# Two-part gather and scatter in the experts, earlier expert loads, and a modulation in halves, in a two-block transformer kernel

## The reference

```python
sh1, sc1, g1, sh2, sc2, g2 = split(silu(c) @ w_mod + b_mod, 6)        # and the same for c_ctx
hx = rmsnorm(x, norm_attn_g) * (1 + sc1) + sh1                        # hc: the same of ctx
proj = hx @ w_in                                                      # queries, latents, keys, values
x = x + g1 * (attention over 256 context and 256 own tokens) @ w_out
t = rmsnorm(x, norm_ffn_g) * (1 + sc2) + sh2
combine = softmax weights of the 2 best of 4 experts in the best of 4 groups, 0 elsewhere   # [256, 16]
hid = silu(t @ w_gate[e]) * (t @ w_up[e])                             # for each of 16 experts
y = sum over e of (hid * combine[:, e]) @ w_down[e]
x = x + g2 * y
```

## Time and profile before

| | us |
|---|---|
| median of three runs | 817.56 |
| lowest, highest | 816.85, 819.56 |
| the profiled execution's own time | 819.27 |
| its span in the trace | 817.5 |

### The profile page before, as it was taken

One profiled execution on the slowest core, in us unless ns is written; L12 is line 12 of the kernel. 1 busy time (PEld: TensorE's weight loads), 2 busy tenths in 40 slices (PEclk: granted clock), 3 DMA queues, 4 the chain that ended last, 5 costly groups with the idle time before them and its releaser, 6 DMA issues.

```text
span 817.5 us, 12040 instructions
## 1 busy us (share of the span) xinstructions
PE 780.9 (96%) x4707; PEld 561.6 (69%) x4708; DVE 396.3 (48%) x710; ACT 309.5 (38%) x564; POOL 22.5 (3%) x22
## 2 busy tenths in 40 slices
PE   4899999998998999999999999999899999999997
PEld 2588885443794544553554458887798999999885
DVE  0685504579744111110111136776646788888543
ACT  2453203556523101110110134655445666666433
POOL 0000020022000000000000000020000000000000
PEclk9999999999999999999999997999996999999999
DMA  9935012977259999999999994203402445575301
GB/s 378 420 124 213 21 83 103 350 279 280 95 220 382 396 422 422 421 422 422 422 422 423 421 429 176 103 1 135 201 2 93 152 169 205 205 307 223 139 1 51
DMA packets 22549, 198.89 MB, mean 243 GB/s; under 512 B 2512, under 2 KB 2896, under 8 KB 3952
## 3 DMA queue, kind: packets, MB, share of 16 engines
q1 hardware_dynamic: 21600, 194.80, 59.6%
q0 software_dynamic: 624, 3.28, 1.0%
q10 hardware_dynamic: 288, 0.30, 0.1%
HBM read 197.31 MB, written 1.05 MB: 243 GB/s over the span
## 4 chain that ended last, share of the span: by engine, by line
PE 86%; DVE 6%; DMA 4%; ACT 3%; issue 1%; DVEq 0%; SPq 0%; ACTq 0%
PE banks L1400 13%; PE banks L1040 9%; PE banks L1656 7%; PE banks L1426 7%; PE banks L1631 6%; PE banks L1639 5%; PE banks L1635 5%; PE banks L1365 4%; PE banks L1376 4%; PE banks L1188 2%; PE banks L981 2%; DMA ring<-in_w_in 2%; DVE w_lo L1705 2%; PE banks L1066 2%; PE banks L1070 2%; PE banks L1068 2%
## 5 line engine op out<-in xcount | busy, mean ns | idle before, releaser
L1705 DVE TENSOR_TENSOR w_lo<-ring,w_hi 128x1024 fp32r<-128x1024 f32 x119 | 145.0, 1225 | 80.8 <-ACT w_hi L622 32.7
L1400 PE MATMUL banks<-ring,att 128*64 128x512 f32 x512 | 111.3, 592 | 1.9 <-DVE att L2013 1.9
L1400 PEld LDWEIGHTS banks<-ring,att 128*64 128x64 f32 x512 | 36.9, 137 | 74.4 <-issue 74.4
L622 ACT ACTIVATE w_hi<-ring 128x1024 fp32r<-128x1024 f32 x53 | 55.0, 1054 | 42.8 <-PE banks L1040 28.3
L1426 PE MATMUL banks<-ring,att 128*64 128x512 f32 x256 | 56.7, 595 | 0.6 <-DVE att L2030 0.6
L2028 DVE TENSOR_TENSOR att<-att,banks 128x512 f32<-128x512 f32 x8 | 5.5, 688 | 98.7 <-PE banks L1400 98.7
L1631 PE MATMUL banks<-h_hi,w_hi 128*128 128x256 f32 x352 | 52.3, 292 | 0.3 <-ACT h_hi L916 0.3
L893 ACT ACTIVATE w_hi<-ring 128x1024 fp32r<-128x1024 f32 x44 | 46.2, 1053 | 15.1 <-PE banks L1639 15.1
L1639 PE MATMUL banks<-h_lo,w_hi 128*128 128x256 f32 x352 | 50.2, 286 | 0.0
L1635 PE MATMUL banks<-h_hi,w_lo 128*128 128x256 f32 x352 | 50.2, 286 | 0.0
L1631 PEld LDWEIGHTS banks<-h_hi,w_hi 128*128 128x128 f32 x352 | 47.4, 197 | 1.3 <-issue 0.6
(11 more groups left out here) (341 smaller groups left out, 1379.6 us busy)
## 6 DMA issues: line engine op xcount, KB each, us to landing
ring<-in_w_down SPq DMA_DIRECT2D x33, 1024.0 KB, 11.5
ring<-in_w_gate SPq DMA_DIRECT2D x32, 1024.0 KB, 12.4
ring<-in_w_up SPq DMA_DIRECT2D x32, 1024.0 KB, 15.7
ring<-in_w_mod SPq DMA_DIRECT2D x12, 2048.0 KB, 9.9
ring<-in_w_up SPq DMA_DIRECT2D x11, 2048.0 KB, 7.7
ring<-in_w_in SPq DMA_DIRECT2D x8, 2048.0 KB, 13.5
ring<-in_w_down SPq DMA_DIRECT2D x5, 2048.0 KB, 10.8
ring<-in_w_out SPq DMA_DIRECT2D x4, 2048.0 KB, 7.9
```

What stands on the lines that cost most here:

```text
L622: nc.scalar.activation(chunk_part(w_hi, chunk, c), chunk_src(chunk, c), ACT.Copy).then_inc(chunk_hi[stage], 1)
L1400: last = nc.tensor.matmul(bank[2 + j][CAP * e:CAP * (e + 1), :], xs[:, k, CAP * e:CAP * (e + 1)], slot(n + e, KD)[:, k, :], start=(k == 0) ...
L1705: return V.tensor_tensor(dst, src, high.bitcast(F32), ALU.subtract)
```

## The change

It has three parts.

1. **Start.** The four pieces of w_mod come in the order 0, 2, 1, 3, so that the first two hold scale and shift of the row blocks 0 to 3, and the other two those of 4 to 7. Two pieces share a bank, and `mod_pick` turns both at once. The weights of `ql` come in two halves, the first ahead of w_mod. DVE and ACT make `mod`, `A1`, `hT_hi`, `hT_lo` and the split of `ql` by halves, and PE forms all three ql products by halves too (`latent_q`): the first half between the second and the third piece of w_mod. The squares of x are summed ahead of the first piece. Those of the context are made on ACT, added up on DVE over the row blocks, and need one matmul. Short bf16 matmuls (`stay_awake`) stand at places where PE would wait. In `PROD` naq comes ahead of kvl. The third piece of w_mod is loaded to `arena`.
2. **Experts.** The tokens are kept in two parts, `h2tok_hi` (ACT) and `h2tok_lo` (DVE, in the memory of `h2_lo`), and the gather multiplies both with `picks_r`, for four experts (two pairs) at once: 256 columns. It stands in the second pair of two, in halves (L1479 of the changed kernel). The result of a pair is written in two parts, `ysb_hi` and `ysb_lo`, scaled by the slot's weight (`slot_w`), and the scatter multiplies both with a `place` of zeros and ones (L1465). `place` and `slot_w` are made by DVE from the transposed `pick_w`.
3. **Loads.** The first pair's four down pieces go to other memory (`spare`: `big`, `arena`, `mixT`), three of them as soon as the first attention has ended. The second pair's down pieces are then issued ahead of its gate pieces. The first gate pieces no longer wait for w_out. `sgw` of the second block is loaded after the experts.

Core of the diff:

```diff
-L_QL, L_KVL, L_NAQ, L_NAK, L_NAV, L_UQ, L_UKV = range(4, 11)
+L_QL, L_MOD, L_NAQ, L_KVL, L_NAK, L_NAV, L_UQ, L_UKV = 0, 1, 5, 6, 7, 8, 9, 10
+MOD_ORDER = (0, 2, 1, 3)
...
+            def query_weights(half, done):
+                cols = slice(half * KD // 2 * QL, (half + 1) * KD // 2 * QL)
+                sp.dma_start(home(L_QL)[:, cols], w_in_part("ql")[0][:, cols]).then_inc(done, 16)
+
+            query_weights(0, landed_later[slot_of(L_QL)])
+            issue(L_MOD, w_mod[MOD_ORDER[0]])
+            issue(L_MOD + 1, w_mod[MOD_ORDER[1]])
             sp.dma_start(ctxT, ctxT_d).then_inc(in_ctx, 16)
-            issue(L_QL, *w_in_part("ql"))
+            issue(L_MOD + 2, w_mod[MOD_ORDER[2]])
+            issue(L_MOD + 3, w_mod[MOD_ORDER[3]])
+            query_weights(1, landed[slot_of(L_QL)])
+            issue(L_NAQ, *w_in_part("naq"))
             issue(L_KVL, *w_in_part("kvl"))
             sp.dma_start(con[:, CON_FIRST:NCON], con_d[:, CON_FIRST:NCON]).then_inc(in_rest, 16)
-            issue(L_NAQ, *w_in_part("naq"))
             sp.dma_start(row[:, :], row_d.broadcast_to([P, NROW])).then_inc(in_row, 16)
             sp.dma_start(wr[:, :, :], wr_d).then_inc(in_row, 16)
...
+            def expert_load(i, j, done=None):
+                stage, half, e = j // 4, j // 2 % 2, j % 2
+                n = L_MOE + 2 * stage + e
+                cols = slice(half * SLOT // 2, (half + 1) * SLOT // 2)
+                dst, landed_at = ring[:, slot_of(n), cols], (landed, landed_later)[half][slot_of(n)]
+                if done is not None:
+                    dst, landed_at = done
+                sp.dma_start(dst, (w_gate, w_up, w_down)[stage][i * 2 + e][:, cols]).then_inc(landed_at, 16)
+
+            def spare_load(j):
+                half, e = j // 2 % 2, j % 2
+                expert_load(0, j, (spare(e, half), landed_spare[half]))
+
+            def expert_loads(i, before, js=range(12)):
+                for j in js:
+                    sp.wait_ge(used, before + (j + 1))
+                    expert_load(i, j)
+
+            sp.wait_ge(*through(last_in_slot(L_MOE)))
+            expert_load(0, 0)
+            expert_load(0, 2)
+            sp.wait_ge(ATT[0]["pv"], 8)
+            for j in (8, 10, 11):
+                spare_load(j)
+            for j in (1, 3, 4, 6):
+                if j in (1, 4):
+                    sp.wait_ge(*through(last_in_slot(L_MOE + 2 * (j // 4) + j % 2)))
+                expert_load(0, j)
+            sp.wait_ge(proj_out, KD)
+            for j in (5, 7):
+                expert_load(0, j)
+            spare_load(9)
+            for j in range(8, 12):
+                expert_load(1, j)
+            expert_loads(1, 0, range(8))
+            with sp.Fori(0, NPAIR - 2) as i:
+                expert_loads(i + 2, i * 12 + 12)
...
-            pool.wait_ge(ATT[0]["pv"], 4)
+            pool.wait_ge(logits_part, 1)
+            pool.dma_start(wr[:, :, :], wf_d).then_inc(in_wf, 16)
+            pool.wait_ge(resid_m, 1)
...
-                inputs(w * 16 + 1)
-                with act.Fori(0, NPAIR - 1) as i:
-                    pair(i)
-                pair(NPAIR - 1, last=True)
+                    if gathers:
+                        inputs(w * 16 + d * 4 + 5, 0, 0)
+                    act.wait_ge(place_done, w * 8 + d * 2 + (odd + 1))
+                    act.wait_ge(used, w * 96 + d * 24 + (12 * odd + 10))
+                    act.wait_ge(scattered, w * 8 + d * 2 + (odd + 2))
+                    nc.scalar.activation(ysb_hi[:, 0:512], bank[2][:, :], ACT.Identity, scale=slot_w[:, odd:odd + 1]
+                                         ).then_inc(y_hi, 1)
...
+            def latent_q(half):
+
+                for part, x in ((w_hi, hT_hi), (w_lo, hT_hi), (w_hi, hT_lo)):
+                    for c in range(3):
+                        if x is hT_hi:
+                            done = (ql_hi, chunk_hi[0])[half] if part is w_hi else (ql_lo, chunk_lo[0])[half]
+                            pe.wait_ge(done, c + 1)
+                        for k in range(4 * half, 4 * half + 4):
+                            if part is w_hi and c == 0:
+                                pe.wait_ge(shifted if x is hT_hi else shifted_lo, k + 1)
+                            last = nc.tensor.matmul(bank[c][:, 0:T], chunk_part(part, CHUNK1, c)[:, k, :], x[:, k, 0:T],
+                                                    start=(part is w_hi and x is hT_hi and k == 0),
+                                                    stop=(x is hT_lo and k == KD - 1))
+                        if x is hT_lo and half == 1:
+                            last.then_inc(prod_ready, 1)
...
+            pe.wait_ge(silu_c, 1)
+            pe.wait_ge(in_con, 16)
+            pe.wait_ge(first_sq, 1)
+            for k in range(KD):
+                last = nc.tensor.matmul(bank[7][:, 0:T], ones, hT[:, k, 0:T], start=(k == 0), stop=(k == KD - 1))
+            last.then_inc(sumsq, 1)
+            mod_stream(L_MOD, 4, 0, True, False)
+            mod_stream(L_MOD + 1, 4, 2, False, True)
+            stay_awake(3, 3)
+            mod_pick(0)
+            stay_awake(5, 3)
+            latent_q(0)
+            mod_stream(L_MOD + 2, 5, 0, True, False)
+            pe.wait_ge(ctx_added, 3)
+            nc.tensor.matmul(bank[7][:, T:2 * T], ones, hT[:, 0, T:2 * T], start=True, stop=True).then_inc(sumsq, 1)
+            stay_awake(4, 3)
+            mod_stream(L_MOD + 3, 5, 2, False, True)
+            stay_awake(3, 3)
+            mod_pick(1)
+            stay_awake(5, 3)
+            latent_q(1)
+
...
+            def scatter(odd, ms, final=False):
+
+                for m in ms:
+                    for part in (ysb_hi, ysb_lo):
+                        last = nc.tensor.matmul(yacc(m), part[:, m * P:(m + 1) * P], place[:, odd, :],
+                                                start=False, stop=False, skip_group_check=True)
...
+                def gather(d, b, ks, parts):
+
+                    for part in parts:
+                        for k in ks:
+                            dst = bank[b + (k - ks[0]) // 2][:, k % 2 * T:(k % 2 + 1) * T]
+                            for q in range(NT):
+                                last = nc.tensor.matmul(dst, part[:, q, k * P:(k + 1) * P],
+                                                        picks_r[:, bass.ds(d * 256 + q * 1024, T)],
+                                                        start=(part is h2tok_hi and q == 0 and k % 2 == 0),
+                                                        stop=(part is h2tok_lo and q == NT - 1), skip_group_check=True)
+                            if part is h2tok_lo and k % 2 == 1:
+                                last.then_inc(gathered, 1)
...
+            modulation(0)
+            scaled_by_norm(0, range(4))
+            shifted_low(0, range(4))
+            dve.wait_ge(first_sq, 2)
+            for i, n in enumerate((4, 2, 1)):
+                if i:
+                    dve.wait_ge(ctx_added, i)
+                V.tensor_tensor(hT[:, 0:n, T:2 * T], hT[:, 0:n, T:2 * T], hT[:, n:2 * n, T:2 * T], ALU.add
+                                ).then_inc(ctx_added, 1)
+            first_rstd(1)
+            queries_to_lo(1, (0,))
+            modulation(1)
+            scaled_by_norm(0, range(4, KD))
+            queries_to_lo(1, (1, 2))
+            shifted_low(0, range(4, KD))
+            chunk_to_lo(0, CHUNK1, 3)
 
...
+                def result_low(d, odd, half):
+                    at = slice(512 * half, 512 * (half + 1))
+                    dve.wait_ge(y_hi, w * 16 + d * 4 + (2 * odd + half + 1))
+                    V.scalar_tensor_tensor(ysb_lo[:, at], bank[2 + half][:, :], slot_w[:, odd:odd + 1],
+                                           ysb_hi[:, at].bitcast(F32), ALU.mult, ALU.subtract).then_inc(y_lo, 1)
+
```

479 lines of the change are left out of this document (260 added, 219 removed).

## The result

The changed kernel takes 808.26 us, the median of four runs (807.70 to 808.44), beside 818.07 for the kernel before (816.85 to 819.56). The ratio is 0.9885, 95% interval 0.9862 to 0.9909: faster by 9.8 us. The forecast was 799.7 with a range of 793.8 to 807.2. The direction and the bound of the experts' stage were right; a good half of the forecast gain arrived.

What follows compares the result with a forecast made beforehand. PE and DMA were both full in the experts' stage, with DMA setting the end. Terms -5.9 (start), -13.0 (experts) and +1.0 (behind) sum to -17.9, taking the median of 817.56 to 799.7, range 793.8 to 807.2.

Steps and rivals of the forecast that it cites:

- What bounds the kernel.: Experts' stage, 258 to 489: PE and DMA both full, with loads at 29.8 a pair slower than PE at 28.63.
- The experts' term, -13.0.: Experts' stage: DMA sets the end, down products end at 471.4 instead of 484.4; bounds 10.5 to 15.5.
- The margin of 4.4: Experts' early loads: they fill the queue until 284.5, leaving 4.4 before the third pair's first gate piece would move.
- The term behind, +1.0.: Behind the experts, last down products to the residual's norm sum: 10.7 instead of 9.7, range 0 to +3.
- The start's term, -5.9.: Start, to the end of the three ql products: 41.9 instead of 47.8; bounds 2.9 to 8.3.
- "The attention behind is the same work by its own waits, and moves forward as a whole.": Attention after the start: unchanged work that passes on the start's whole gain; forecast change 0.
- "without a gap of note": Reading of the profile before: from the end of the ql products at 47.79, PE is busy.
- "I cost this edit at nothing": First gather before the experts: ACT's four extra copies lie beside the gather, so the first gate products stay at 258.4.
- Rival 1: Start: ql halves run at 1.2 GHz, so the gain is only 0 to 2, time 804 to 806; chance 0.15.
- Rival 3: Experts from the sixth pair: PE waiting for loads falls to the lower clock, making the kernel slower than before; chance 0.04.
- The range.: Whole kernel: 793.8 to 807.2, from bounds of 2.9 to 8.3, 10.5 to 15.5 and 0 to 3.

Runs made afterwards that it cites:

- the last two kernels: Changed kernel with all waits filled behind which the clock fell and POOL's sums in four pieces, 799.59; then all helpful edits together on the changed kernel, 795.89.
- part 1 alone: The kernel before with only the start's change (halves, order of projections): 814.92 us, ratio 0.9959.

## Why the prediction was wrong, step by step

- **What bounds the kernel.** Right. Two resources full at once, DMA the one that does not give way: half the bytes make the stage 10.4 shorter, and PE's own time is 203.7 against the 201.2 in the working. The path at the very end was another one: PE's last wait for a load is for an up piece of the last pair (1.32 at 458.8), while the last down piece lands 0.6 before it is read.
- **The experts' term, -13.0.** Right in size: -12.25. The pairs are 23.26, 27.68 and 24.34 for 23.2, 27.2 and 24.1. The margin of 4.4 in which the queue was to be idle was a dry spell of some 2.5 instead, and it cost about that: removing it gave 2.45.
- **The term behind, +1.0.** At its own place it is +2.0, inside its range of 0 to 3. That the whole rest of the program comes to +0.8 is luck, since stretches at half speed lie elsewhere in the two executions. Its larger half was a wait that I named only in passing, DVE behind ACT's rounding; reordering it gave 2.4, more than the term. One reading was off: the last down products of before end at 484.8 (477.73 + 7.09), not 484.4. The 0.4 moves from this term to the experts' and leaves the sum as it is.
- **The start's term, -5.9.** The mechanism was right and the size was off: -3.4. Of the 2.5, 1.5 is the second stream at half speed. I had taken 1.9 for it, from a row at full clock, though a wait for a load stands ahead of it. About 0.5 is the landing of its load, 18.3 for 17.8.
- **"The attention behind is the same work by its own waits, and moves forward as a whole."** This is the step that failed. It lost 2.8 in the profiled execution: 0.85 and 0.25 to the two meetings of DVE and POOL at 163 and 182, 1.6 to the clock at 209. It is not even the same work: POOL's sum takes 0.7 longer wherever part 1 is in. The rest is not new. The waits were in the trace of before (0.34, 2.06 and 1.12); I read "without a gap of note", and did not list them.
- **"I cost this edit at nothing"**, the first gather. With the making of `picks_r` it cost 0.96, a term that was named as open ("if DVE is later by some time, the start is later by that time") and then left out of the bounds.
- **Rival 1** had a part of the cause, half speed, at the wrong place: not in the ql products, whose waits were filled, but at a stream and in the attention. It did not have POOL. **Rival 3** did not come: in the experts' stage the clock is 1.00 from 260 to 460, with waits of up to 1.3 for loads between bursts. Its 55 us carried over a case whose waits are longer than the 1.5 forecast here, as the last section says.
- **The range.** 808.26 lies 1.1 above it. Its upper end let the start fail by 3.0 and the rest by 4.5, but held no case in which work that the change does not touch loses time.

What stays open: which of two equal waits is followed by a fall, and why POOL's sums are longer with part 1. Executions of the same instructions differ in the falls. Ahead of the experts the clock stayed full in the profiled executions of the last two kernels, and over their ten runs the mean granted clock is 0.986 to 0.998, for 0.98 in the changed kernel; a filling of two waits only moved the falls. No run has the fillings without POOL's pieces, or the pieces without the fillings.

## What to carry to other kernels

A gain early in a program reaches the end only through every wait behind it, so list these waits in the trace of before, with what ends each and which other engine is busy there, and put a price on each of meeting differently. Where a later stage is bound by loads whose issue waits for PE's reading, what counts is when that stage begins: one us earlier there was one us at the end (2.96 to 2.8). Here the largest price was DVE held behind a long POOL instruction: in four pieces it gave 3.5 of the 6.0 us that were won ahead of the experts. Filling PE's waits with matmuls on zeros is the second means, and it pays only where the falls do not find another wait: two filled waits gave nothing; all those behind which a fall had been seen, with POOL's pieces, gave 8.7. And compare the length of an instruction before and after even where the change leaves its line alone.

## What the runs showed of the hardware that I had not expected

- **The same code at either clock.** The product behind the wait of 1.12 at 207 to 212 ran at half speed (1.2 GHz) in four of nine executions and at full speed (2.4 GHz) in five. Waits up to 2.61 were followed by full speed in some places (187.20 with part 1 alone) and by half speed in others (18.16 in the same execution); each fall cost 1.4 to 1.6. The second stream took 3.44 in the changed kernel and 1.92 in three kernels whose instructions up to there are the same, but there the wait ahead of it was shorter. The Trainium skill, TensorE: Matmul & The Clock Gate, HAM oscillation, tells of a kernel whose waits of 3 to 5 us for loads put every burst of matmuls at half speed. No wait here is in that range once the first load has landed. The trace adds that 1.12 can be enough, and that in the experts' stage waits of up to 1.3 for loads did nothing (clock 1.00 from 260 to 460).
- **DVE held by POOL.** Two scalings of a [128, 512] float32 tile from memory to memory take 0.88 alone and 4.63 beside one POOL sum of 4.53; the second of them ends 0.7 behind it. With POOL's work in four pieces of 1.3 they took 2.21. The Trainium skill, GPSIMD Engine Reference, Specifications, says that the two engines share their interfaces to SBUF, with contention when DVE runs in a two-port mode or has two inputs there. The trace agrees that they contend, though it does not show in which mode DVE ran; and it adds how much: DVE is held for the rest of POOL's instruction.
- **One POOL instruction, two lengths.** The same sum over [128, 2048] float32 took 4.51 to 4.76 in eight kernels and 3.80 to 3.97 in two, with the mask's columns in `con` two further on in the eight. That this is the cause is not shown.
- **A queue that has run dry** takes some time to fill again: from 284 to 288.5 it moved 100 GB/s on average, though pieces were issued from 285.81 on (the first landed at 290.66), and 422 from 288.5 on.
